# Prompt scores moved beside the second unit's value products, value rows kept in the query's buffer, further interruptions joined

## The reference, cut to what matters

```python
D_MODEL, SEQ, DEC_BATCH, PAST_LEN, PAGE_SIZE = 2048, 512, 8, 2048, 128
HEAD_DIM, N_ATT_HEADS, N_LRU_BLOCKS, CONV_W = 128, 8, 8, 4
xn = rms_norm(x, g_mix)
z = jnp.einsum('btd,dc->btc', xn, w_in)          # [q | k | v | forget logits | x-branch | gate-branch]
logf = log_sigmoid(f_logit + b_f)
# attention: 8 heads; the samples read their cached pages too
s = q.k / sqrt(d) + F[t] - F[s], causal;  p = softmax(s);  att = p @ v
# recurrent group: 8 blocks
xc = causal_conv(xl, conv_buf, w_conv, b_conv)
r, i = sigmoid(xc @ wa + ba), sigmoid(xc @ wx + bx)
a = exp(-8 * r * softplus(-lam));  h_t = a*h_{t-1} + sqrt(1 - a*a)*(i*xc)
lru = gelu(gl) * h
x = x + concat(rms_norm(att), rms_norm(lru)) @ w_out
x = x + square(relu(rms_norm(x) @ w_up)) @ w_down
y = rms_norm(x, g_final)
```

## Time and profile before

| what | value |
|---|---|
| median of 3 runs | 2286.39 us (2285.51 to 2286.99) |
| the profiled execution | 2287.92 us, its span 2286.3 us |
| granted TensorE clock | 0.994 of full speed |
| TensorE busy | 2245.4 us, 98% of the span |
| DVE, ACT, POOL busy | 1605.0, 858.7, 154.1 us (70%, 38%, 7%) |
| HBM traffic | 161 GB/s mean |

### The profile page before, as it was taken

How to read it: one execution, slowest core, us unless ns; L and a number is a source line. 1 busy time by engine, 2 the same in 40 slices (tenths; PEclk the granted TensorE clock), 3 DMA queues, 4 the chain that set the end, 5 groups by cost and what they waited for, 6 DMA issues and landing times.

```text
span 2286.3 us, 50021 instructions
## 1 busy us (share of the span) xinstructions
PE 2245.4 (98%) x19889; PEld 2197.9 (96%) x19889; DVE 1605.0 (70%) x2043; ACT 858.7 (38%) x1201; POOL 154.1 (7%) x194
## 2 busy tenths in 40 slices
PE   7999999999999999999999999999999999999997
PEld 6999999999988999999999999999999999999997
DVE  7349999999984697767576566566566566566563
ACT  5224434343454333343243243243243243243245
POOL 0001111111113031000000000000000000000002
PEclk8999999999999999999999999999999999999998
DMA  6358999999965242333333433433433433433422
GB/s 236 100 161 259 342 336 345 325 323 327 336 238 199 95 148 81 93 114 104 116 111 100 120 110 93 127 110 89 131 110 86 134 107 86 137 101 92 138 91 95
DMA packets 386972, 368.47 MB, mean 161 GB/s; under 512 B 12259, under 2 KB 350596, under 8 KB 385844
## 3 DMA queue, kind: packets, MB, share of 16 engines
q1 hardware_dynamic: 359828, 295.38, 42.2%
q0 software_dynamic: 18608, 67.64, 8.1%
q10 hardware_dynamic: 8448, 4.20, 0.6%
HBM read 354.22 MB, written 12.94 MB: 161 GB/s over the span
## 4 chain that ended last, share of the span: by engine, by line
PE 93%; DVE 3%; ACT 2%; DMA 1%; SPq 1%; issue 0%; DVEq 0%; ACTq 0%
PE PS L1897 40%; PE PS L1901 20%; PE PS L2343 9%; PE PS L2342 9%; PE PS L2341 9%; PE PS L2058 2%; PE PS L2085 1%; PE PS L2106 1%; DVE WL L1214 1%; PE PS L2248 1%; ACT WH L744 0%; PE PS L2096 0%; DMA VR<-in_cache_v 0%; SPq L439 0%; DMA RAW<-in_w_in 0%
## 5 line engine op out<-in xcount | busy, mean ns | idle before, releaser
L1094 ACT ACTIVATE WH<-RAW 128x1024 fp32r<-128x1024 f32 x293 | 304.9, 1057 | 680.8 <-PE PS L1901 521.4
L1648 DVE TENSOR_TENSOR WL<-RAW,WH 128x1024 fp32r<-128x1024 f32 x293 | 358.1, 1222 | 134.4 <-ACT WH L1094 132.8
L1897 PE MATMUL PS<-XH,WH 128*128 128x260 f32 x1952 | 405.2, 289 | 12.4 <-DVE XL L1279 7.2
L1897 PE MATMUL PS<-HH,WH 128*128 128x260 f32 x2048 | 412.5, 282 | 1.4 <-DVE HL L1653 0.7
L1901 PE MATMUL PS<-HH,WL 128*128 128x260 f32 x2048 | 411.6, 282 | 0.0
L1897 PE MATMUL PS<-HL,WH 128*128 128x260 f32 x2048 | 410.9, 282 | 0.0
L1901 PE MATMUL PS<-XH,WL 128*128 128x260 f32 x1952 | 394.1, 283 | 0.0
L1897 PE MATMUL PS<-XL,WH 128*128 128x260 f32 x1952 | 393.8, 283 | 0.0
L1751 DVE TENSOR_TENSOR A<-A,PS 128x520 f32<-128x520 f32 x256 | 177.3, 695 | 264.5 <-PE PS L1901 264.2
L1897 PEld LDWEIGHTS PS<-XH,WH 128*128 128x128 f32 x1952 | 301.9, 189 | 23.2 <-issue 12.2
L1897 PEld LDWEIGHTS PS<-HH,WH 128*128 128x128 f32 x2048 | 314.6, 188 | 2.1 <-issue 1.1
(11 more groups left out here) (335 smaller groups left out, 3082.8 us busy)
## 6 DMA issues: line engine op xcount, KB each, us to landing
KR<-in_cache_k POOLq DMA_DIRECT2D x128, 512.0 KB, 6.1
VR<-in_cache_v SPq DMA_DIRECT2D x128, 512.0 KB, 5.9
RAW<-in_w_up SPq DMA_DIRECT2D x128, 512.0 KB, 4.2
RAW<-in_w_down SPq DMA_DIRECT2D x128, 512.0 KB, 4.4
RAW<-in_w_in SPq DMA_DIRECT2D x82, 512.0 KB, 8.0
RAW<-in_w_out SPq DMA_DIRECT2D x32, 512.0 KB, 5.3
TMP<-in_w_up SPq DMA_DIRECT2D x30, 512.0 KB, 6.0
xT_spill<-A SPq DMA_DIRECT2D x1, 4160.0 KB, 16.4
```

What stands on the lines that cost most here:

```text
L1094: nc.scalar.activation(RING_H[SLOT[i]], RB[b], ACT.Copy).then_inc(f_hi, 1)
L1648: V.tensor_tensor(RING_L[SLOT[i]], RB[op_block(i)], RING_H[SLOT[i]].bitcast(F32), ALU.subtract).then_inc(f_lo, 1)
L1897: mm(dsts[c], wh(k), x[:, k, c * HT:(c + 1) * HT], start=first and n == 0 and x is xh, stop=False)
```

## The change

On TensorE these places move in the steps 1 to 7 (in step 0 only the gate sums):

| work | before | after |
|---|---|---|
| `queries`, `max_rows` | (0, 13), (0, 15) | the same |
| older `values`, `max_all` | (0, 21) | the same |
| `scores`, then `value_cols` | (1, 5) | (1, 21), `value_cols` first, ahead of `values` |
| `values` of pages 0 to 3 | (1, 21) | the same |
| `transpose_probs` | (2, 15) | (2, 21), behind `values` |
| `values` of pages 4 to 7 | (2, 21) | the same |
| `attend` | (2, 27) | (3, 7), ahead of `rows` |
| `rows` | (3, 7) | the same |
| `values` of pages 8 to 11 | (3, 21) | the same |
| gate sums | after the fourth unit | (3, 21), behind `values` |

On DVE, in steps with a previous head: page 4 is scored ahead of `row_maxima`, pages 5 and 6 behind it, page 7 behind `normalized`; pages 12 and 13 are scored behind `conv` and the fourth `split_lo` of the step instead of ahead of them. On ACT the value tile is copied out and the next WH made ahead of `transposed`; the x-branch is copied out and the WH after it made ahead of `attended`; `values_in_place` goes ahead of the copy of kT. `vT` is now `qcur`, so ACT waits for the transposes of the values before it writes the key rows there.

```diff
-        vT = PR[:, 0:SEQ]
+        vT = qcur
...
                 if prev:
                     probabilities(i - 1)
+                if prev and older:
+                    values_in_place(i - 2)
...
-                if prev and older:
-                    values_in_place(i - 2)
                 if prev:
                     softmax(i - 1)
-                if prev:
-                    transposed(i - 1)
                 if head:
                     rows_out(tile_wait(U_L + 1, 2 * i), vT, VS, i)
                     split_hi(U_L + 3, 2 * i)
                 if prev:
-                    attended(i - 1)
+                    transposed(i - 1)
...
                     split_hi(U_L + 4, 2 * i)
-
+                    if prev:
+                        attended(i - 1)
+
+                    act.wait_ge(vtr_ps, i + 1)
...
                 if prev:
+                    if head:
+                        score(i, range(4, 5))
                     row_maxima(h)
...
-                    score(i, range(4, 6))
+                    score(i, range(5 if prev else 4, 7))
                 if prev:
                     denominators(h)
                 if prev:
                     normalized(h)
                 if head:
-                    score(i, range(6, 8))
+                    score(i, range(7, 8))
...
-                    if prev:
-                        score(i, range(12, 14))
                     conv(i)
...
                     split_lo(U_L + 4, 2 * i)
-                    if not prev:
-                        score(i, range(12, 14))
+                    score(i, range(12, 14))
...
                 def head_scores():
                     if head:
                         pe.wait_ge(qb_ready, i + 1)
+                    if older:
+                        value_cols(i - 2)
                     pe.wait_ge(shifted, i)
                     scores(i - 1)
-                    if older:
-                        value_cols(i - 2)
...
+                extra = {}
+                if head:
+                    extra[3, 21] = gate_sums
+                    if not prev:
+                        extra[1, 5] = other_rows
+                    extra[0, 13 if prev else 5] = queries
+                    extra[3, 7] = (lambda: (attend(i - 1), rows())) if prev else rows
+                if prev:
+                    extra[0, 15] = lambda: max_rows(i)
+                    extra[0, 21] = lambda: max_all(i)
+                    extra[2, 21] = lambda: transpose_probs(i - 1)
...
+                    if prev and (q, n) == (1, 21):
+                        f.append(head_scores)
```

More of the change, by code:

```diff
@@ L2202, in rows, with gate_sums @@
                     ins.then_inc(vtr_ps, 1)
+                def gate_sums():
+                    pe.wait_ge(gw_full, 32 * (i + 1))
+                    pe.wait_ge(conv_done, i + 1)
+                    if prev:
+                        pe.wait_ge(att_ready, i)
+                    pe.wait_ge(ktok_ready, i + 1)
+                    pe.wait_ge(vtok_ready, i + 1)
+                    for g in range(2):
+                        mm(PS[:, 4 + g, :], GW[:, g, :], XC[:, 0:SEQ], start=True, stop=True)
+                    for g in range(2):
+                        ins = mm(PS[:, 6, g * NB:(g + 1) * NB], GW[:, g, :], XC[:, SEQ:T], start=True, stop=True)
+                    ins.then_inc(gates_ps, 1)
                 extra = {}
                 if head:
+                    extra[3, 21] = gate_sums
                     if not prev:
@@ L2209, in step @@
                     extra[0, 13 if prev else 5] = queries
-                    extra[3, 7] = rows
+                    extra[3, 7] = (lambda: (attend(i - 1), rows())) if prev else rows
                 if prev:
@@ L2213, in step @@
                     extra[0, 21] = lambda: max_all(i)
-                    extra[1, 5] = head_scores
-                    extra[2, 15] = lambda: transpose_probs(i - 1)
-                    extra[2, 27] = lambda: attend(i - 1)
+                    extra[2, 21] = lambda: transpose_probs(i - 1)
                 def places(q, n):
                     f = []
+                    if prev and (q, n) == (1, 21):
+                        f.append(head_scores)
                     if prev and (q, n) in VALUES_AT:
@@ L2238, in step @@
                         unit(U_L + q, 2 * i, U_L + q, 2 * i, insert)
[L2239 to L2251, removed]
             pe.wait_ge(cum_ready, 3)
```

## The result

| kernel | median of its runs | against the kernel before on the same chip |
|---|---|---|
| before | 2287.08 us (2285.51 to 2287.91, 6 runs) | 1 |
| changed | 2295.32 us (2294.34 to 2296.44, 6 runs) | 1.0034 [1.0023, 1.0046] |

The changed kernel is 8.2 us slower, 0.34%, and stands 2.0 us above the forecast of 2293.3. The sign and both places of the loss are as forecast; some sizes are not. The kernel before has a median of 2287.08 us here, 0.7 above the 2286.39 that the forecast started from, so that in medians 0.7 of the 2.0 us lie in the base and 1.3 in the change (8.2 instead of 6.9).

A forecast was written before the change was run, and what follows sets the result against it. TensorE, busy 98% of the span, was taken as the bound; 2.28 + 2.60 + 0.11 + 1.93 = +6.9 us on the profiled 2287.92 gave 2294.8, median 2293.3 us. Range 2290.5 to 2296; 8 in 10, 2287.5 to 2297.5.

The forecast's parts named there:

- The sign: Whole kernel: the change makes it slower, median 0.30% up; slower by over 0.2% was given 0.76.
- both places of the loss: TensorE's new wait for the fourth unit's split, and the Sigmoid made later by gate sums ahead of Gelu.
- Part 2: `attend` moved behind the fourth split: TensorE arrives sooner and waits 0.74 us for DVE; loop period grows 0.52 us.
- first rival: Fourth unit: the split is not waited for, so not slower; 2285.6 us, or 2283.7 without the end; chance 0.14.
- Part 1: TensorE's interruptions go from eleven to seven a step, saving exits of 0.08 or 0.11 us: 0.38 us a step.
- second rival: TensorE's switches: each costs more than its exit, 0.2 us for each of 28 removed; 2280.8 us; chance 0.07.
- Part 3: Gate sums ahead of Gelu delay ACT's Sigmoid: hidden in steps 2 to 7, +0.23 us in step 1, +1.93 after step 7.
- third rival: ACT's chain overtakes DVE in the loop: each loop step 1.3 us more, about 2299.8 us; chance 0.07.
- Part 4: Other moves (`scores`, convolution, ACT's wait for value transposes, WH, `vT` in `qcur`): each worth 0, up to 1 us a step if uncovered.
- The base: Starting time: profiled execution of 2287.92 us taken as 1.5 above the median of the runs.

The follow-up runs named there:

- E1: Changed kernel with the fourth `split_lo` one key page earlier on DVE, ahead of page 9: 2288.42 us, 1.0003 of the kernel before.
- E2: Changed kernel with `attend` alone put back to (2, 27), ahead of the fourth unit: 2288.91 us, 1.0006 of the kernel before.
- E5: Changed kernel with the fourth unit's `split_lo` one key page later, behind page 10: 2314.71 us, 1.0121 of the kernel before.
- E9: E1 with the four joined pairs of interruptions taken apart by a slice each, eleven a step instead of seven: 2289.41 us, 1.0010 of the kernel before.
- E3: Changed kernel with the gate sums alone put back behind the fourth unit: 2291.96 us, 1.0021 of the kernel before.
- E6: E1 with ACT's Gelu of the fourth unit moved behind the gates' Sigmoid and Tanh, ahead of Exp: 2284.86 us, 0.9989 of the kernel before.
- E7: E6 with Sqrt ahead of the second output unit's WH on ACT, after step 7 only: 2283.93 us, 0.9987 of the kernel before.
- E8: Changed kernel with the fourth split one page earlier in step 1 alone: 2292.86 us, 1.0026 of the kernel before.
- E4: Changed kernel with E1 and E3 together, split one page earlier and gate sums behind the unit: 2287.40 us, 1.0000 of the kernel before.

## Why the prediction was right, and which terms were mis-sized

**Part 2 (a wait for the fourth split) held.** E1 and E2 remove it from either side, E5 makes it larger by a page. The first rival, that the split is not waited for, is out. Its size was a little too large, see Part 1.

**Part 1 (0.38 us a step from fewer switches) was four to five times too large.** The price of an exit was read rightly, but a joined block does not save it whole. In step 6 of the changed kernel:

```profile
550.17 0.40 PE L1901 MATMUL PS<-XH,WL 128*128 128x260 f32 x2
550.41 0.51 PE L2067 MATMUL PS<-ident_r,VOS 128*128 128x4 f32 x4
550.77 0.47 PE L2085 MATMUL PS<-kT,qcur 128*128 128x128 f32 x2
...
554.14 1.93 PE L2058 MATMUL PS<-VR,PP 128*1 128x128 f32 x64
556.00 0.51 PE L1897 MATMUL PS<-XH,WH 128*128 128x260 f32 x2
556.34 0.40 PE L1897 MATMUL PS<-XL,WH 128*128 128x260 f32 x2
```

The block runs from a first product at 550.41 to 556.00, 5.59 us; apart, the two took 3.60 and 1.86, 5.46 together. 0.13 comes back inside it. The other three joins (2.93, 2.95 and 4.04 us, against 2.87, 2.87 and 3.94 apart) give back 0.06, 0.08 and 0.10. So 0.37 of the 0.38 is lost again. What the prediction left out gives 0.09 back: value products begin 0.33 behind the pair before them instead of 0.24, and at (1, 21) `value_cols` now comes first and begins 0.24 behind its pair (550.17 to 550.41). By these starts 0.10 a step is saved; by the periods it is 0.08 (E1), and 0.11 where the pairs are taken apart again (E9). The second rival, that a switch costs more than its exit, is wrong in the other direction: E9 gives 0.03 for one.

This has two effects on the period. Without a wait TensorE would start the fourth unit at 574.08 + 0.24 = 574.32, 46.30 into the step, not 46.18. And DVE ends the split at 46.85, not 46.92. So the unit starts 574.92 - 574.32 = 0.60 late, where the forecast had 0.74 + 0.06 = 0.80. (The listed wait of 0.45 counts from the end of the last pair, 574.08 + 0.40; it is not the distance that the prediction worked with.) The first pair takes 0.35 instead of 0.24, and together that is the 65.75 - 65.05 = 0.70 us of E1. The other effect is that the switches give back only 0.08 of it, not 0.38. So the period grows by 0.70 - 0.08 = 0.62, where 0.90 - 0.38 = 0.52 was forecast. Both terms were too large and nearly cancelled; that is luck.

**Part 3 (gate sums ahead of Gelu) held.** It is hidden in the loop with 0.23 us left, and costs 0.81 in step 1 and 1.77 of the listed wait at the end (E3). E6 and E7 show that ACT's order at the end set all of that wait, also the 2.0 us that before had. The third rival, ACT's chain overtaking DVE, is out: the Sigmoid stands 2.12 into the step, where 2.14 was worked out with 0.04 of hidden time. Left out of the forecast were the 0.24 us of the first output unit.

**The term that was missing is TensorE's clock behind a standstill.** Step 1 came 1.24 us dearer than forecast. With E8's 62.77 and the 0.26 that a wait costs beside its listed length (E3: 62.77 + 1.07 + 0.26 = 64.10, as measured), a wait of 1.88 gives 64.91; measured 66.43. The stretches of the changed kernel around it (us, then busy time and count of PE, PEld, DVE, ACT, POOL, granted clock, DMA share, GB/s):

```profile
240.00:244.60 4.60, 2.75 (x23) 2.54 (x22) 4.57 (x4) 1.81 (x4) 1.05 (x2) 1.00 1.00 396
244.60:249.20 4.60, 4.58 (x25) 4.58 (x26) 4.53 (x4) 0.71 (x1) 0.53 (x1) 0.63 1.04 384
```

And its matmuls there:

```profile
245.98 0.64 PE L1901 MATMUL PS<-XH,WL 128*128 128x260 f32 x2
246.41 0.64 PE L1897 MATMUL PS<-XH,WH 128*128 128x260 f32 x2
246.84 0.64 PE L1897 MATMUL PS<-XL,WH 128*128 128x260 f32 x2
```

A granted clock of 0.63 is a mean over a stretch at 1.2 GHz and one at 2.4: the pairs keep to 0.24 us for the first 1.3 us behind the wait and then follow each other after 0.43 until 249.0. That is the 1.5 us. In the trace of before the stretches around the fourth unit of step 1 were granted 1.00. That the standstill brought the clock down is supported by E8, whose step 1 has neither; but not every standstill of this size does so (last section).

The 1.24 hides a second miss. In step 1 the forecast had a wait of 2.5 us (2.56 with its 0.06); by starts the unit came at 244.62 where 242.35 + 0.24 = 242.59 was open to it, 2.03 late. The trace of before has a pause of DVE just ahead of this split, for a DMA of keys, that the prediction did not see and that is not in the changed kernel's trace:

```profile
241.37 1.23 DVE L1350 TENSOR_TENSOR KR<-KR,QB 128x1024 f32<-128x1024 f32 x1 [0.32 <-DMA KR<-in_cache_k]
```

So the wait was 0.5 us shorter than forecast, the switches saved 0.14 instead of 0.38 (62.91 against E8's 62.77), and the clock added 1.5: 1.2 us in all.

**Part 4 held.** No other new wait is listed, and E4 is at 1.0000. What it costed at nothing did not show.

**The base.** The forecast took the median to be 1.5 us below the profiled execution; that of the changed kernel is 0.2 above it. Counted that way, this is 1.7 of the 2.0 us missed. The other 0.3 is 7.2 against 6.9, where a head start of 1.9 us in the profiled execution hides most of the 2.2 by which the stages were costed too low. That the difference of the two profiled executions came out so close to 6.9 is luck.

## What to carry to other kernels

When work of the engine that is hardly ever idle is moved behind a point where it meets another engine, subtract the moved work from the slack there before counting what it saves: here 2.08 us were moved against 1.61 us of slack, and placing one page of DVE's work (2.4 us) behind the split instead of ahead of it repaired it. Cost the last iteration of a loop by itself, since what is hidden inside the loop (the gate sums ahead of Gelu) stands in the open at its end. And an interruption joined to another is worth its period measured, not its exit.

## What the runs showed of the hardware

**A wait costs more than its listed length.** Where TensorE's matmul stream had to wait, the step grew by 0.25 to 0.26 us beside the wait that the profile lists: 0.45 listed and 0.70 in the period, 1.07 and 1.33 in step 1 (E3), 2.84 and 3.09 in E5. In step 6 of the changed kernel 0.16 of it is the overhang of the last pair (it is listed as 0.40 long, where the next would have begun after 0.24), and 0.11 is the first pair behind the wait.

**The clock falls behind some standstills and not behind others.** In E5 the same wait stands in each step. After that of step 2 and of step 3 the stretches read:

```profile
318.60:323.20 4.60, 4.60 (x25) 4.48 (x26) 4.00 (x8) 0.00 (x0) 0.53 (x1) 0.68 1.05 384
388.10:392.70 4.60, 4.60 (x29) 3.86 (x30) 4.00 (x8) 0.00 (x0) 0.53 (x1) 1.00 1.03 395
```

Their waits are 2.85 and 2.84 us, and 1.4 us of period lie between the two (69.51 and 68.14). The waits of 2.84 or 2.85 in steps 4 to 7 were followed by a granted clock of 1.00. The waits for WL at a fourth unit and for the XL of block 7, from 0.45 us up, in the traces:

| listed wait | where | granted clock behind it |
|---|---|---|
| 0.45 to 0.57 | steps 2 to 6: changed, E3, E8; step 7: E3 | no pair slower than at full clock |
| 1.07 | step 1: E3 | full |
| 1.88 | step 1: changed | low, 1.3 us behind it |
| 2.03, 2.03, 2.04 | the end: before, E3, E4 | full; low, 1.4 us behind it; low at once |
| 2.84 to 2.85 | steps 2 to 7: E5 | low at once in step 2, full in five |
| 3.78 to 3.83 | the end: changed, E1, E2, E5, E8, E9 | low in all six, at once or up to 1.3 us behind it |
| 4.21 | step 1: E5 | low, 1.1 us behind it |

Low is 0.50 of full speed, 1.2 GHz. What decides it between 1.88 and 2.85 us isn't settled by these runs. It cost 1.4 to 1.6 us more than the standstill in the three steps where that was measured (step 1 of the changed kernel, steps 1 and 2 of E5). It may be part of the 2 to 4 us between runs of one kernel: in the 33 runs of the kernel before on one chip the longer ones have the lower mean granted clock (correlation -0.6). A run's record doesn't say where the clock was lost.
